# Nine RMS norms whose eighth square TensorE sums, and VectorE's last product issued ahead of the final norm's multiplications

## The reference

```python
def rms_norm(x, w):
    xf = x.astype(jnp.float32)
    y = xf * lax.rsqrt(jnp.mean(xf * xf, axis=-1, keepdims=True) + NORM_EPS)
    return (y * w.astype(jnp.float32)).astype(x.dtype)
...
    hid = jax.nn.silu(jnp.einsum('becd,edf->becf', xe, w_gate)) * jnp.einsum('becd,edf->becf', xe, w_up)
    ye = jnp.einsum('becf,efd->becd', hid, w_down) * top_aff[..., None].astype(h.dtype)
    combine = lambda ib, yb: jnp.zeros((L, D), yb.dtype).at[ib.reshape(-1)].add(yb.reshape(-1, D))
...
        x = x + g2 * expert_choice_ffn(h, w_router[l], w_gate[l], w_up[l], w_down[l])
    return rmsnorm(x, norm_f)
```

## Time and profile before

| | us |
|---|---|
| median of 3 runs | 3171.93 (3171.75 to 3174.51) |
| the profiled execution | 3174.3 |
| its span in the trace | 3172.5 |
| mean granted TensorE clock in it | 0.97 of full |

### The profile page before, as it was taken

How to read it: one execution, slowest core, us unless ns; L and a number is a source line. 1 busy time by engine, 2 the same in 40 slices (tenths; PEclk the granted TensorE clock), 3 DMA queues, 4 the chain that set the end, 5 groups by cost and what they waited for, 6 DMA issues and landing times.

```text
span 3172.5 us, 41633 instructions
## 1 busy us (share of the span) xinstructions
PE 2996.2 (94%) x17048; PEld 2328.3 (73%) x17048; DVE 1664.1 (52%) x3194; ACT 1064.3 (34%) x2151; POOL 176.4 (6%) x149
## 2 busy tenths in 40 slices
PE   8999999989999999999999899999899997988887
PEld 7888778878888888888888778888687986333333
DVE  6876674465655655555663655445654674122112
ACT  4222354453332343333453642222333552000002
POOL 0000002230000000000002220000001100000000
PEclk9999999999999999999999999999899888999999
DMA  5554411112223221222211113222111006999997
GB/s 218 192 186 183 149 67 42 49 57 93 103 93 123 93 80 68 89 79 71 93 54 49 41 58 113 100 93 93 70 67 54 2 3 260 410 421 421 421 421 322
DMA packets 66310, 444.40 MB, mean 140 GB/s; under 512 B 7492, under 2 KB 7748, under 8 KB 19656
## 3 DMA queue, kind: packets, MB, share of 16 engines
q1 hardware_dynamic: 62600, 428.89, 35.3%
q0 software_dynamic: 1696, 6.55, 0.6%
q10 hardware_dynamic: 1824, 6.29, 0.5%
HBM read 436.20 MB, written 5.51 MB: 139 GB/s over the span
## 4 chain that ended last, share of the span: by engine, by line
PE 77%; DVE 9%; DMA 6%; ACT 4%; SPq 3%; issue 1%; POOL 0%; ACTq 0%; DVEq 0%
PE ps L181 76%; DMA b<-in_eg 5%; DVE b L201 5%; DVE b L191 3%; SPq L155 3%; ACT b L207 2%; PE ps L312 1%; ACT b L414 1%; DVE b L196 1%; POOL b L191 0%; DMA b<-in_wu 0%; DMA b<-in_xt 0%; ACT L207 0%; ACT b L206 0%; DVE b L2062 0%
## 5 line engine op out<-in xcount | busy, mean ns | idle before, releaser
L181 PE MATMUL ps<-b,b 128*128 128x512 f32 (+9 forms) x13750 | 2711.4, 386 | 128.2 <-DVE b L191 30.1
L181 PEld LDWEIGHTS ps<-b,b 128*128 128x128 f32 (+5 forms) x13750 | 2073.2, 183 | 731.3 <-issue 296.1
L191 DVE TENSOR_TENSOR b<-b,b 128x512 f32<-128x512 f32 (+9 forms) x726 | 620.9, 860 | 303.2 <-ACT b L414 183.1
L414 ACT CAST b<-b 128x1024 fp32r<-128x1024 f32 (+2 forms) x408 | 392.0, 963 | 387.4 <-PE ps L181 300.5
L191 DVE TENSOR_TENSOR b<-ps,b 128x64 f32<-128x64 f32 (+5 forms) x607 | 209.4, 359 | 250.4 <-PE ps L181 195.0
L181 PE MATMUL ps<-b 64*64 64x64 f32 (+10 forms) x2848 | 247.9, 276 | 17.4 <-DVE b L2062 6.0
L181 PEld LDWEIGHTS ps<-b 64*64 64x64 f32 (+3 forms) x2848 | 211.7, 160 | 50.4 <-issue 18.7
L207 ACT ACTIVATE b<-b 128x512 f32<-128x512 f32 (+7 forms) x288 | 153.1, 538 | 225.5 <-DVE b L201 179.5
L191 POOL TENSOR_TENSOR b<-b,b 128x1024 fp32r<-128x1024 f32 (+3 forms) x96 | 142.4, 1503 | 1326.6 <-ACT b L414 921.7
L191 DVE TENSOR_TENSOR b<-b,ps 128x512 f32<-128x512 f32 (+1 forms) x114 | 77.1, 678 | 236.9 <-PE ps L181 233.9
L201 DVE SCALAR_TENSOR_TENSOR b<-b,b 128x512 f32<-128x512 f32 (+7 forms) x300 | 176.9, 601 | 44.7 <-ACT b L207 40.3
(11 more groups left out here) (105 smaller groups left out, 541.8 us busy)
## 6 DMA issues: line engine op xcount, KB each, us to landing
b<-in_eg SPq DMA_DIRECT2D x64, 1024.0 KB, 27.1
b<-in_eu SPq DMA_DIRECT2D x64, 1024.0 KB, 26.3
b<-in_ed SPq DMA_DIRECT2D x64, 1024.0 KB, 26.7
b<-in_wg SPq DMA_DIRECT2D x44, 1024.0 KB, 4.8
b<-in_wu SPq DMA_DIRECT2D x44, 1024.0 KB, 4.8
b<-in_win SPq DMA_DIRECT2D x40, 1024.0 KB, 4.8
b<-in_wd SPq DMA_DIRECT2D x48, 768.0 KB, 4.3
b<-in_wmod SPq DMA_DIRECT2D x24, 1024.0 KB, 5.8
```

The source lines that it names most:

```text
L181: return e.h.matmul(out, l, r, start=start, stop=stop)
L191: return e.h.tensor_tensor(out, a, b, op)
L414: e.h.copy(hi, src).then_inc(*self.S.tick(("hi", i)))
```

## The change

**In all nine norms**, VectorE's eighth addition is gone (`stat_dve` returns for k = 7). TensorE sums `nacc` and the eighth square in `two[1]` in pairs that accumulate in PSUM: eight products in place of four (four in place of two for the context). It waits for `("add", 6)` and ScalarE's `("sq", 7)`. Those two take the place of `("add", 7)` in every `ends`.

**In the experts' last pair**, the four multiplications by the norm's weight row become `final_weigh(i)` and leave the loop of half 0: number 0 stands ahead of half 1's `t`, number 1 between `t` and `ylo`, numbers 2 and 3 behind `ylo`.

```diff
     def stat_dve(self, e, k, src):
-        if k == 0:
+        if k in (0, 7):
             return
...
-    def norm_sum(self, e, bank, n, there):
-        e.wait_ge(there)
+    def norm_sum(self, e, bank, n, src):
+        one = self.k.K["one"][:, 0:1]
+        e.wait_ge(src.V.at(("add", 6)), src.S.at(("sq", 7)))
         for t in range(n // 128):
-            p = mm(e, bank[:, t:t + 1], self.nacc[:, t * 128:t * 128 + 128], self.k.K["one"][:, 0:1])
+            c = slice(t * 128, t * 128 + 128)
+            mm(e, bank[:, t:t + 1], src.nacc[:, c], one, True, False)
+            p = mm(e, bank[:, t:t + 1], src.two[1][:, c], one, False, True)
         p.then_inc(*self.P.tick("norm"))
...
-        self.ends = [(self.V, ("add", 7)), (self.P, ("sum", self.mine[-1]))]
+        self.ends = [(self.V, ("add", 6)), (self.S, ("sq", 7)), (self.P, ("sum", self.mine[-1]))]
...
         for h in range(2):
             cs, t = slice(h * 512, h * 512 + 512), self.ex[h]
+            if h:
+                self.final_weigh(e, 0)
             e.wait_ge(P.at(("w", 7, 4 + h, 1)), V.at(("hid", 7, h)), S.at(("row", h)))
             stt(e, t, B[4 + h][:, :], self.vT[:, 7:8], self.rows[h], ALU.mult, ALU.mult).then_inc(*V.tick(("t", h)))
+            if h:
+                self.final_weigh(e, 1)
             e.wait_ge(S.at(("yhi", h)))
             tt(e, self.ylo[:, cs], t, self.yhi[:, cs].bitcast(F32), ALU.subtract).then_inc(*V.tick(("ylo", h)))
+            if h:
+                self.final_weigh(e, 2)
+                self.final_weigh(e, 3)
             for i in range(4):
                 x = self.xt[i][:, cs]
                 e.wait_ge(P.at(("z", h, i)), S.at(("xt", h, i)))
                 tt(e, x, x, self.zbank(h, i)[:, :], ALU.add).then_inc(*V.tick(("x", h, i)))
-                if h == 0:
-                    e.wait_ge(V.at(("x", 0, i)), S.at(("row", 2)), P.at(("w", 7, 3, 0)))
-                    tt(e, self.out[:, i, 0:512], x, self.rows[2], ALU.mult).then_inc(*V.tick(("n", i)))
...
+    def final_weigh(self, e, i):
+        e.wait_ge(self.V.at(("x", 0, i)), self.S.at(("row", 2)), self.P.at(("w", 7, 3, 0)))
+        tt(e, self.out[:, i, 0:512], self.xt[i][:, 0:512], self.rows[2], ALU.mult).then_inc(*self.V.tick(("n", i)))
```

More of the change, by code:

```diff
@@ L478, in stat_dve, with norm_pe @@
         tt(e, acc, acc, self.two[k % 2][:, 0:src.shape[1]], ALU.add).then_inc(*self.V.tick(("add", k)))
-    def norm_pe(self, e, bank, n, there):
-        self.norm_sum(e, bank, n, there)
+    def norm_pe(self, e, bank, n, src):
+        self.norm_sum(e, bank, n, src)
         self.norm_spread(e, bank, n)
-    def norm_sum(self, e, bank, n, there):
-        e.wait_ge(there)
+    def norm_sum(self, e, bank, n, src):
+        one = self.k.K["one"][:, 0:1]
+        e.wait_ge(src.V.at(("add", 6)), src.S.at(("sq", 7)))
         for t in range(n // 128):
-            p = mm(e, bank[:, t:t + 1], self.nacc[:, t * 128:t * 128 + 128], self.k.K["one"][:, 0:1])
+            c = slice(t * 128, t * 128 + 128)
+            mm(e, bank[:, t:t + 1], src.nacc[:, c], one, True, False)
+            p = mm(e, bank[:, t:t + 1], src.two[1][:, c], one, False, True)
         p.then_inc(*self.P.tick("norm"))
@@ L586, in __init__ @@
         self.dx = [k.count(f"in_x{i}") for i in range(4)]
-        self.ends = [(self.V, ("add", 7))]
+        self.ends = [(self.V, ("add", 6)), (self.S, ("sq", 7))]
     def x_there(self, c):
@@ L1242, in pe @@
             self.host.enter(e)
-            self.norm_pe(e, B[6], 256, V.at(("add", 7)))
+            self.norm_pe(e, B[6], 256, self)
         elif name == "small":
@@ L1443, in pe @@
                     e.wait_ge(self.before.dma["k_const"].at(0))
-                self.norm_pe(e, k.bank[7], 512, self.before.V.at(("add", 7)))
+                self.norm_pe(e, k.bank[7], 512, self.before)
             elif name == "sum":
@@ L1605, in __init__ @@
         self.number()
-        self.ends = [(self.V, ("add", 7)), (self.P, ("sum", len(self.items) - 1))]
+        self.ends = [(self.V, ("add", 6)), (self.S, ("sq", 7)), (self.P, ("sum", len(self.items) - 1))]
     XB = (2, 3, 6, 7)
@@ L1831, in pe @@
                 self.enter(e)
-                self.norm_sum(e, B[7], 512, self.before.V.at(("add", 7)))
+                self.norm_sum(e, B[7], 512, self.before)
             elif name == "sum" and i == 0:
@@ L2602, in pe @@
             if name == "norm":
-                self.norm_pe(e, B[7], 512, self.before.V.at(("add", 7)))
+                self.norm_pe(e, B[7], 512, self.before)
             elif name == "sum":
@@ L2762, in __init__ @@
         self.number()
-        self.ends = [(self.V, ("add", 7)), (self.P, ("sum", 7))]
+        self.ends = [(self.V, ("add", 6)), (self.S, ("sq", 7)), (self.P, ("sum", 7))]
     def sp(self, e):
@@ L3102, in pe @@
         self.enter(e)
-        for t in range(4):
-            p = mm(e, B[7][:, t:t + 1], k.nacc[:, t * 128:t * 128 + 128], k.K["one"][:, 0:1])
-        p.then_inc(*P.tick("norm"))
+        self.norm_sum(e, B[7], 512, self.before)
         for m in range(8):
```

## The result

The changed kernel takes 3178.78 us in the median (3172.81 to 3181.65, 20 runs), the kernel before beside it 3172.15 us (3166.24 to 3176.14, 20 runs). The ratio is 1.0021, 95% interval [1.0014, 1.0027]: slower by 6.6 us, within the predicted range and 2.8 us above the predicted 3176.0. The profiled execution took 3179.36 us, with a span of 3177.6 us.

What follows compares the result with a forecast made beforehand. TensorE was taken to bound the kernel, busy 2996.2 of 3172.5 us. 5.4 + 0 - 0.7 + 0.4 - 1.05 = +4.05 us on the median of 3171.93 gave 3176.0 us, range 3171.8 to 3180.0.

Steps and rivals of the forecast that it cites:

- The price of the added sums: Six norms where TensorE arrives late: eight more passes cost 0.9 us each, +5.4 us in all.
- The context: Norm at 777 us: 0.45 us more of sums fits into TensorE's 1.22 us of idling, so 0.
- `Mixer2`, -0.7 us: Norm at 2241 us: without the addition VectorE's clearing starts sooner, so the mean comes 0.6 to 0.85 us sooner.
- The experts' norm, +0.4: Norm at 2671 us: sums start 0.5 us sooner but take 0.9 us more; ends +0.3 and +0.6.
- The end, -1.05: Experts' last pair: moved multiplications let `t` of half 1 start right behind TensorE's product; -0.7 to -1.7 us.
- The sum: All terms over the whole kernel: +4.05 us on the median, giving 3176.0 us; chance 0.62.
- the clock falling at more norms: Rival: longer low-work stretches halve TensorE's clock, 1.7 us a fall; two falls 3179.4, three 3181.1 us; chance 0.18.
- VectorE's chain gave back: Rival: the removed addition saves time at all eight full norms, 6.8 us less, 3165.1 us; chance 0.03.
- the last sums lost nothing to the moved multiplications: Denies a rival: at the experts' end the moved multiplications delay the sums, 0 gained, 3177.0 us; within the 0.62.
- nearly-free rival: All norms: TensorE overlaps or takes up the added passes, 0.2 us a norm, -0.3 us, about 3171.6; chance 0.13.
- the own range of the sum: Whole kernel: ends of the terms and one clock fall more or less, stated as 3173.8 to 3178.2 us.

Runs made afterwards that it cites:

- e6_mix2: Kernel before plus the moved multiplications, with the eighth square summed by TensorE in `Mixer2` alone; ratio to the kernel before 0.9992 [0.9982, 1.0002].
- the second comparison: The changed kernel itself, run again beside the kernel before on another experiment's chip; 3178.14 us, ratio 1.0017 [1.0008, 1.0027].
- e2_norms: The changed kernel with the moved multiplications undone, so only the nine norms differ from the kernel before; 3181.73 us, ratio 1.0034.
- e9_shift: Kernel before with only the spread of the four feed-forward norms put behind six 128x512 passes of the next product; ratio 0.9975, 6 runs.
- e11_shift_again: Kernel before with only the four feed-forward norms' spread put behind six 128x512 passes, repeated with 11 runs; ratio 0.9991 [0.9980, 1.0002].
- e4_four: Kernel before, eighth addition kept, with each of the norms' summing products issued four times; 3208.09 us, ratio 1.0120 to the kernel before.

## Why the prediction was right, and where it was off

**The price of the added sums, 0.9 us in six norms: right for the feed-forward norms.** It was 0.89 at 722 us by the traces (2.07 less 1.18 us), for the reason given: TensorE arrives late, and the removed addition gives nothing back. For the two mixers' norms the price is not shown by itself: the stretches behind them differ by more from one execution to the next. Sixteen passes took 1.8 us, and a step stays 0.11 us. The 25 ns of the Trainium skill ("TensorE: Matmul & The Clock Gate", "Back-to-back issue gap") were no rule for these passes: the same section gives them for an isolated product and says that they leave out the weight load, which each of these passes has.

**The context, 0: right.** The 0.45 us fitted into TensorE's wait ahead of the spread.

**`Mixer2`, -0.7 us: right in mechanism, but it hangs on the clock.** In the changed kernel the mean came 0.65 us sooner. The spread ran at full clock there as well, and the root started 1.56 us behind the mean instead of 2.49, 0.93 us more; the prediction had left this to the range. In e6_mix2 the clock fell inside the sums and 0.2 us of it came.

**The experts' norm, +0.4: right.** From VectorE's last product to the mean it is 3.79 us, against 3.35 before, and TensorE goes into the sums without a wait.

**The end, -1.05: mechanism right, size off.** `t` starts directly behind TensorE's product, as forecast. The step "TensorE's `z` for half 1 starts 1.04 us sooner ... and the first sum follows it by 2.50 us as before" was wrong in its second half: TensorE now idles 1.50 us in place of 2.52, its clock stays at the full level, and `z` is ready before the moved multiplications are done. The end came 1.72 us sooner, which the prediction had as the bound of this term.

**The sum.** With the measured terms it is 5.3 - 0.65 + 0.44 - 1.72 = +3.4 us; the median moved by 6.6 us, the second comparison by 5.4. What is missing is the rival that had been given 0.18, the clock falling at more norms. The step of the prediction that failed is the argument against this rival, "sums of 0.9 us are not idling": it took one-column passes for work that keeps the clock up. The counts above show 1.5 falls in an execution at the feed-forward norms, none with eight passes, which is 2.6 us and brings the sum to +6.0, or +5.1 where `Mixer2`'s spread has the full clock; the measured intervals are 4.4 to 8.6 and 2.5 to 8.6. The falls and their price are read from traces; that they make up all of the difference is an agreement of sizes, within these intervals. The rival's own figure for two falls, 3179.4, was nearer to the result than my forecast. The three others fell: nothing was taken up (the 0.47 us stayed), VectorE's chain gave back at `Mixer2` only, and the last sums lost nothing to the moved multiplications. Two recorded sums don't come out as written. The -0.2 in the nearly-free rival is not derived; at its own 0.2 us a norm the experts' term gives 0.7 us less than in the main sum, so 3171.1 and not 3171.6. And the ends of the terms, with 1.7 us for a fall either way, give 3173.1 to 3178.6, wider than the stated 3173.8 to 3178.2.

The median lies in the predicted range, but 0.6 us above the own range of the sum: what held it is the room left for two falls, and the end's extra 0.67 us, which hid part of them.

**What stays open.** Why the clock falls at one norm of 16 passes and not at the next was not settled. Nor was why e2_norms has so much more time at half clock than before. In its profiled execution it is 205.7 us against 190.0: two falls at feed-forward norms make 6.8 of it, and the largest other part is the stretch behind the experts' norm, 46.4 us against 34.3. But e9_shift and e11_shift_again, with eight passes at that norm, have 46.1 us there. Whether the changed norms shift the falls in other stages was not tested.

## What to carry to other kernels

Moving an addition from an idle engine to the bottleneck engine costs its full price wherever the bottleneck arrives late, so look at which engine's wait ends last at each place, and make the change only there: in `Mixer2` it brought the mean 0.65 us forward while the clock held, at six other norms it cost some 0.9 us each. Reckon very narrow passes on TensorE not only by their time: a run of them may halve the clock for the work behind it (for 3.4 us here); with wide passes put between them and the spread no fall was seen at four feed-forward norms. At a program's end, order a queue by what the next engine waits for; that gain is small (1.7 us by the local reading), but little stands behind it that could take it back.

## What the runs showed of the hardware

One-column fp32 passes with their own weight loads, issued without a gap, can be followed by a fall of the granted clock. At the feed-forward norms it fell to 0.50 behind 0.9 us of them at none of 32, behind 1.8 us at 6 of 16, and behind or within 3.6 to 4.1 us (e4_four) at 4 of 4. In e4_four it fell at the five other norms too; at three of those (389 us, `Mixer2`, the experts) it falls in some executions with eight passes as well. The Trainium skill ("TensorE: Matmul & The Clock Gate", "What's actually happening") ties the clock to how busy the engine has lately been. The busy time in the traces does not tell the falls apart: TensorE is shown busy without a break up to the falls at 32.1 and 1138.0 us of e4_four.
